# One step of a decoder trunk: the S5 outputs and two attention weighings a tile later in the input projection

## What is computed

```python
ada = cond @ w_ada[l] + b_ada[l]
h = x * (1.0 + scale[:, None]) + shift[:, None]
proj = h @ w_in[l]
y_a = a_b * causal_dwconv(a_c * a_x, conv_a[l]) * jax.nn.silu(a_g)
y_b = dilated_attention(q, k, v, rel_bias) * jax.nn.silu(b_g)
y_c = rglru_branch(c_x, ...) * jax.nn.silu(c_g)
# s5_branch: y = Re(C x) + D u
y = jnp.einsum('gcp,bsgp->bsgc', c_re, x_re) - jnp.einsum('gcp,bsgp->bsgc', c_im, x_im)
y = y.reshape(Bsz, S, BR) + d_skip * u
x = layer_norm(ALPHA * x + (1.0 + gate[:, None]) * (concat(y_a, y_b, y_c, y_d) @ w_out[l]), ...)
```

## Time and profile before

| what | value |
| --- | --- |
| median of 3 runs | 1693.5 us (1692.15 to 1694.27) |
| the profiled execution | 1694.41 us |
| its span, first to last instruction | 1692.6 us |
| mean granted TensorE clock | 0.989 of full |
| PE busy | 1636.2 us, 97% |
| VectorE, ScalarE, GpSimd busy | 1172.4, 759.2, 177.5 us |
| chain that ended last | PE 81%, DVE 9%, DMA 6% |
| moved by DMA | 372.01 MB, 220 GB/s |

### The profile page before, as it was taken

One profiled execution on the slowest core, in us unless ns is written; L12 is line 12 of the kernel. 1 busy time (PEld: TensorE's weight loads), 2 busy tenths in 40 slices (PEclk: granted clock), 3 DMA queues, 4 the chain that ended last, 5 costly groups with the idle time before them and its releaser, 6 DMA issues.

```text
span 1692.6 us, 22915 instructions
## 1 busy us (share of the span) xinstructions
PE 1636.2 (97%) x7708; PEld 1266.6 (75%) x7708; DVE 1172.4 (69%) x2335; ACT 759.2 (45%) x994; POOL 177.5 (10%) x242
## 2 busy tenths in 40 slices
PE   5799999999999999999999999999999999999996
PEld 0347777778777777788887777777877777778885
DVE  1438976985796598668867884687388468753758
ACT  1336535554654455521127554654555465442212
POOL 2001111111111111000000111111111111100000
PEclk9899999999999999999999999999999999999998
DMA  9999899999999998878748888888988888776524
GB/s 364 358 310 229 215 225 267 221 206 239 242 226 233 246 221 199 212 275 269 236 144 212 204 199 193 207 202 205 220 204 198 190 208 201 189 185 242 180 99 113
DMA packets 316866, 372.01 MB, mean 220 GB/s; under 512 B 30536, under 2 KB 227488, under 8 KB 314080
## 3 DMA queue, kind: packets, MB, share of 16 engines
q1 hardware_dynamic: 288608, 270.57, 49.8%
q0 software_dynamic: 27504, 100.15, 33.4%
q10 hardware_dynamic: 656, 0.17, 0.0%
HBM read 263.89 MB, written 10.99 MB: 162 GB/s over the span
## 4 chain that ended last, share of the span: by engine, by line
PE 81%; DVE 9%; DMA 6%; issue 2%; ACT 1%; SPq 0%; DVEq 0%; ACTq 0%
PE bank L1332 19%; PE bank L1285 17%; PE bank L1295 17%; PE bank L1286 17%; DMA pro<-in_w_ada 3%; DVE work L1671 3%; DMA w_lo<-raw 1%; PE bank L1196 1%; DVE y_t L1679 1%; PE bank L1222 1%; PE bank L974 1%; PE bank L1210 1%; DVE ada_acc L1679 1%; PE bank L1161 1%; PE bank L1170 1%
## 5 line engine op out<-in xcount | busy, mean ns | idle before, releaser
L1285 PE MATMUL bank<-op,w_hi 128*128 128x512 f32 x1456 | 579.3, 398 | 0.0
L1286 PE MATMUL bank<-op,w_hi 128*128 128x512 f32 x1456 | 568.1, 390 | 0.0
L702 ACT ACTIVATE w_hi<-raw 128x1024 fp32r<-128x1024 f32 x187 | 198.2, 1060 | 430.5 <-PE bank L1286 256.7
L1295 PE MATMUL bank<-op,w_lo 128*128 128x512 f32 x1456 | 360.2, 389 | 0.6 <-DMA w_lo<-raw 0.5
L1285 PEld LDWEIGHTS bank<-op,w_hi 128*128 128x128 f32 x1456 | 273.4, 188 | 76.6 <-issue 18.8
L1295 PEld LDWEIGHTS bank<-op,w_lo 128*128 128x128 f32 x1456 | 272.9, 188 | 58.8 <-DMA w_lo<-raw 2.1
L1286 PEld LDWEIGHTS bank<-op,w_hi 128*128 128x128 f32 x1456 | 273.5, 188 | 56.8 <-issue 1.9
L631 POOL DMA_DIRECT2D w_lo<-raw x187 | 163.4, 874 | 1312.7 <-ACT w_lo L707 1105.7
L1332 PE MATMUL bank<-w_hi,op 128*128 128x512 f32 x960 | 232.6, 393 | 2.1 <-ACT op L906 2.1
L707 ACT ACTIVATE w_lo<-raw 128x1024 fp32r<-128x1024 f32 x185 | 195.2, 1055 | 85.9 <-PE bank L1295 84.8
L1679 DVE SCALAR_TENSOR_TENSOR ada_acc<-ada_in,cond,ada_acc 128x512 f32<-128x512 f32 x225 | 169.1, 751 | 74.5 <-DMA ada_in<-in_w_ada 55.3
(11 more groups left out here) (258 smaller groups left out, 1496.6 us busy)
## 6 DMA issues: line engine op xcount, KB each, us to landing
raw<-in_w_in SPq DMA_DIRECT2D x192, 512.0 KB, 4.8
w_lo<-raw POOLq DMA_DIRECT2D x187, 512.0 KB, 5.4
ada_in<-in_w_ada SPq DMA_DIRECT2D x256, 256.0 KB, 4.8
pro<-in_w_ada SPq DMA_DIRECT2D x32, 1024.0 KB, 9.6
raw<-in_w_out SPq DMA_DIRECT2D x64, 512.0 KB, 4.4
y_t<-in_x SPq DMA_DIRECT2D x2, 2048.0 KB, 12.8
bias_t<-bias_rows_scratch SPq DMA_DIRECT2D x16, 256.0 KB, 6.0
y_t<-in_x SPq DMA_DIRECT2D x4, 1024.0 KB, 8.1
```

The costliest lines, as they stand in the source:

```text
L702: act.activation(w_hi[:, n % NHL, :], raw[:, n % NRAW, :], ACT.Copy).then_inc(s.hi_done.sem, 1)
L1285: pe.matmul(o, w_hi[:, n % NHL, w], op_hi[k], start=k == 0, stop=False)
L1286: mm = pe.matmul(o, w_hi[:, n % NHL, w], op_lo[k], start=False, stop=False)
L1295: mm = pe.matmul(o, w_lo[:, n % NHL, w], op_hi[k], start=False, stop=k == KT - 1)
```

## The change

In the first step of layer 0 alone, the S5 outputs stand behind tile 20 instead of 19; the second weighing and the last turning behind 21 instead of 20; the last weighing behind 23 instead of 22, ahead of `ada_sum`. All other steps keep their table.

```diff
-                    put(19, s5_outputs)
+                    put(20 if first else 19, s5_outputs)
                     for t, at in enumerate((10, 10, 12, 13)):
                         put(at, scores, t)
                     put(11 if first else 10, v_turn)
-                    for g, (at_turn, at_weigh) in enumerate(((16, 18), (18, 20), (20, 22))):
+                    for g, (at_turn, at_weigh) in enumerate(((16, 18), (18, 21), (21, 23)) if first else ((16, 18), (18, 20), (20, 22))):
                         put(at_weigh, weigh, g)
                         put(at_turn, p_turn, g)
```

## The result

| | median | runs |
| --- | --- | --- |
| before | 1694.3 us | 14 (1692.15 to 1696.56) |
| the change | 1697.24 us | 14 (1692.52 to 1699.22) |

The ratio is 1.0014, with a 95% interval from 1.0007 to 1.0020: 2.4 us over before by the ratio, 1.2 to 3.4 us by its interval, 2.9 us by the medians. The change is slower by something that can be measured, and by no more than the 0.2% of the forecast's "same". The profiled execution took 1696.44 us, its span 1694.7 us.

A forecast was written before the change was run, and what follows sets the result against it. TensorE, busy 97% of the span, was taken to bound the kernel. -1.8 (a) + 1.8 (c) + 0.7 (d, e) = +0.7 us on the profiled 1694.41 gave 1695.1, or 1694.2 as median; range 1691.6 to 1696.8.

The forecast's parts named there:

- same: Whole kernel: measured time within about 0.2%, 3.4 us, of before, which cannot be told from no change; chance 0.91.
- likeliest case: Whole kernel: +0.2 to +1.6 us with no fall of the clock; chance 50%.
- every case but one: The one outside 0.2%: clock falls at tile 22 and the ada sum, ada loads 1.9 us late; +4.8 us, chance 5%.
- (a): Outputs behind tile 20: their 1.8 us wait for VectorE's last state goes; tile 21's w_lo part at 232.9, not 236.36.
- (b): Second weighing and last turning behind tile 21: 1.66 us as before, cost nothing; tile 22 could start its w_lo at 240.0.
- (c): Tile 22: raw still leaves at 227.81, w_lo lands at 242.2, TensorE waits 2.3 us; the gain is spent, change so far 0.
- (d): Last weighing behind tile 23: no longer covered by a wait, costs 0.6 us; TensorE reaches the ada sum at 251.3.
- (e): Outputs' release at 229.2, not 225.6: VectorE 1.9 us later, ada loads late, ada sum at 251.4: +0.7 us (-0.1 to +1.6).
- (f): After the ada sum: no later wait swallows the delay, so nothing gives the 0.7 us back or adds to it.
- its fall: Rival: clock drops to 1.2 GHz once, after idle time at tile 22 or the ada sum; +2.3 us, 1695.8, chance 25%.
- gain kept: Rival: w_lo and ada transfers hurry, up to 2.6 us faster (1690.9), halfway 1692.9; chance of 0.5 us or more 14%.

The follow-up runs named there:

- e2: Against the kernel before: outputs stay behind tile 19, only the weighings and the last turning moved a tile later; ratio 1.0005 (0.9996 to 1.0013).
- e1: Against the change: the last weighing put back behind tile 22, the rest kept; ratio to before 1.0006 (0.9994 to 1.0018).
- e9: The change itself run once more, nothing altered; ratio to before 1.0009 (0.9999 to 1.0019), median 1697.59 us.
- e5: Against the kernel before: TensorE's order untouched, only the signal that the outputs are done raised later, by tile 20; ratio 1.0012 (1.0003 to 1.0020).
- e11: Against the change: ada products 16 to 19 ahead of VectorE's last scan, raw of tiles 22 and 23 loaded ahead of ada tiles 24 to 27; ratio to before 0.9984.
- e3: Against the change: four unread matmuls added ahead of the ada sum's wait in the first step; ratio to before 1.0005, median 1695.7 us.
- e7: Against the kernel before, TensorE's order kept: ada products 16 to 19 ahead of VectorE's last scan, raw of tile 22 loaded earlier; ratio 1.0015 (1.0006 to 1.0024).
- e4: Against the kernel before: four unread matmuls added ahead of the ada sum's wait, as a control; ratio 1.0007 (0.9998 to 1.0015), median 1696.57 us.

## Why the prediction held, and where its size was off

The forecast was +0.7 us and the likeliest case of "within 0.2%"; the ratio says +1.2 to +3.4. The way was right and the size was not. That "same" came true says little for the mechanism, since every case but one of the forecast lay within it. The median of the change, 1697.24, even lies above the upper end of 1696.8; before too measured 0.8 us more in 14 runs than in the three of the forecast (1694.3 against 1693.5), and the difference, +2.9, lies within the +3.3. By its own steps, on the clock of before:

- (a) The wait of 1.8 us gone: so. Tile 20's w_lo part at 225.31 (225.3 forecast), tile 21's at 232.87 (232.9).
- (b) No cost of the second weighing and last turning: so for the change, where tile 22 could start at 239.97 (240.0). The cover was not named in full: e2 shows that ScalarE's copy behind the last turning holds tile 23's split, and costs as soon as the outputs aren't early.
- (c) Raw of tile 22 unmoved at 227.81: exactly. Its w_lo landed 0.8 us sooner than forecast; the transfer took 5.8 us and not 6.5, so tile 22 started at 241.52 (242.3), after 1.5 us in place of 2.3, and only just above the 241.5 below which the prediction called itself wrong. The length of this one transfer scatters, from 5.2 to 7.1 us in the thirteen profiles. The estimate of 3.2 us by the fit of the Trainium skill (DMA: Bandwidth & Descriptors, the anatomy of one DMA) is not seen here: the shortest of the 187 w_lo transfers in before's trace took 4.5 us.
- (d) The last weighing behind its cover: TensorE came to the ada sum's wait at 252.53 - 0.85 - 0.71 = 250.97 (251.3 forecast). True, but not what ends last; e1 takes it back and gains nothing. By (d) the low end of (e) could not be -0.1: TensorE itself would not have been there before 251.3, +0.6.
- (e) The release at 229.2, VectorE 1.8 us late, SP's last group ending at 244.33 (244.4): so. The ada sum started 1.1 us late, and in e9, the same kernel once more, 0.6 us late (251.16 with tile 19 at 219.76), so the forecast +0.7 was a fair size. The way to it was another. The forecast let the last load land and gave VectorE 0.75 us for it; that gives 251.05, as the last load landed at 250.3. But the first of the last four landed 3.9 us late, at 248.4, and VectorE needed 3.32 us for the four in a row, to 251.8. That the middle came out is partly luck.
- (f) Nothing behind it gives anything back: the waits behind are the same; the half clock there varies by itself.
- **The step that missed is the choice of the likeliest case,** in which the clock stayed at full speed; its fall had 25%. Of the 12 profiles of changed kernels, the four in which TensorE waited 0.85 us or more ahead of the ada sum (the change, e1, e5, e9) all have the half clock right behind it, and none of the eight without such a wait has it there. In the change it cost 1.7 us (7.15 us in place of 5.47), in e9 3.3. That rival gave +2.3 us; with the ada term as the first profile has it, it is +1.1 + 1.7 = +2.8, and the ratio's middle is +2.4, the medians +2.9. The rival's price, 1.6 us, was right where the half clock struck once (1.7 us in the change, e1 and e5), and "once TensorE idles there for about 1 us" fits the four waits of 0.85 to 1.43 us. The earlier trace rows gave a reason to rate it higher: both half clocks there stand behind one-column matmuls with an idle time beside them, and the change builds such a pair. They gave no certainty. The pair at the end of layer 0 (idle 0.60 us, in e5 0.75) has the half clock behind it in 7 of the 13 profiles, the one at the end of layer 1 (1.49 us) in 11 of 13, with the same instructions.

In "gain kept", halfway between 1690.9 and 1694.2 is 1692.6, not 1692.9. That rival did not occur with the change: no transfer hurried enough. e11 shows that a gain of its kind is to be had when the loads are moved as well: 2.0 us at the ada sum, where that rival gave 2.6.

## What to carry to other kernels

Moving a late consumer back hides its wait only if nothing hangs on the signal that it gives: write down everyone who waits for that signal, and go one further (here VectorE, then the ring that it frees, then the loads, then the sum at the end of the step). Before taking up a wait of 1.8 us on the main engine, see whether the next tile's data left in time for the main engine to come 1.8 us sooner; if not, move the loads in the same edit, as e11 did. And a new short idle time of TensorE beside its one-column matmuls can cost more than its length, by the half clock behind it: here 0.85 us of waiting were followed by a loss of 1.7 us.

## What the runs showed of the hardware

The granted clock fell to 1.2 GHz behind short idle times. In the four profiles in which TensorE waited 0.85 to 1.43 us ahead of the ada sum's some 2 us of one-column matmuls, 3.4 us at 1.2 GHz followed, in e9 6.8 us. At the ends of the two layers an idle time of 0.60 us behind such matmuls was followed by it in 7 profiles of 13, one of 1.49 us in 11 of 13. Between full matmuls a wait of 2.80 us brought it (e3), one of 2.47 us did not (e1), nor did those of 1.39 and 1.47 us (the change and e9); one of 4.79 us brought 6.8 us of it (e7), and the 1.8 us at the outputs did so in none of four profiles (before, e2, e4, e5). Filling the two idle times of the change with ten matmuls whose result nobody reads made the stretch shorter, by 1.9 us against the change's first profile and by 3.1 us against its second.

Transfers of one size took very different times. The accumulating transfer of tile 22's w_lo, 512 KB, took 5.2 to 7.1 us in thirteen profiles, and the first ada load of the last four, 256 KB, 6.1 us before and 9.0 us when it left 1.0 us later.
